# A gated-convolution and differential-attention block: every engine's order from a build-time list scheduler

## The reference

```python
h = rmsnorm(x, g_mix)
bc, cc, vc, q, k, va, gc, ga = split(h @ w_in)     # 512,512,512,512,512,512,1024,1024
y_c = (bc * causal_dwconv3(cc * vc)) @ w_conv_out
q, k = rope(rmsnorm(q)), rope(rmsnorm(k))          # 4 heads, each 2 sub-heads of 64
p0, p1 = softmax(q_n @ k_n.T / 8), masked by chunks of 64 rows
o = (p0 - lam * p1) @ va                           # 4 heads of 128
y_a = (rmsnorm(o) * 0.2) @ w_attn_out
x = x + (sigmoid(gc + b) * y_c + sigmoid(ga + b) * y_a) @ w_o
gt, up = split(rmsnorm(x, g_ffn) @ w_gate_up)      # 2 x 2816
x = x + (silu(gt) * up) @ w_down
```

## Time and profile before

| | us |
|---|---|
| three runs, median | 2865.08 |
| lowest, highest | 2856.92, 2875.99 |
| profiled execution, span of the slowest core | 2843.8 |
| spans of all eight cores | 2839.7 to 2843.8 |

### The profile page before, as it was taken

The page is one execution under the profiler, slowest core; times in us unless marked ns, Lnnn a source line. Parts: engine busy times, 40 slices in busy tenths (PEclk is TensorE's granted clock), DMA queues, the critical chain, the costliest instruction groups (busy, mean ns, idle before and its releaser), DMA issues.

```text
span 2843.8 us, 41548 instructions; the slowest of 8 cores (2839.7 to 2843.8 us)
## 1 busy us (share of the span) xinstructions
PE 2393.0 (84%) x14080; PEld 1110.5 (39%) x14080; DVE 1159.1 (41%) x2138; ACT 1058.7 (37%) x1556; POOL 243.5 (9%) x239
## 2 busy tenths in 40 slices
PE   2566779886997879987899879998799988999989
PEld 1222334333443334433344334443344444444434
DVE  4445544445344443345333453334533333223444
ACT  2134244223323233332443334443355444555310
POOL 1310110003000020001100021000210000000000
PEclk9788799988999889998999999999999999999999
DMA  6336659851335222352234422244122332223333
GB/s 197 106 126 216 222 164 330 297 174 60 113 118 187 97 82 97 121 174 86 82 104 135 156 68 91 99 143 152 60 90 97 118 127 91 82 78 123 134 120 139
DMA packets 107245, 373.61 MB, mean 131 GB/s; under 512 B 10528, under 2 KB 11680, under 8 KB 103072
## 3 DMA queue, kind: packets, MB, share of 16 engines
q1 hardware_dynamic: 106320, 367.81, 38.6%
q10 hardware_dynamic: 720, 3.15, 0.4%
HBM read 320.58 MB, written 50.33 MB: 130 GB/s over the span
## 4 chain that ended last, share of the span: by engine, by line
PE 67%; DVE 13%; issue 8%; ACT 4%; POOL 4%; DMA 3%; DVEq 1%; ACTq 0%; POOLq 0%; SPq 0%
PE psD L817 20%; PE psD L698 12%; PE psO L617 10%; PE psD L844 9%; PE psS L600 6%; PE psD L515 4%; PE psD L764 4%; PE psD L791 3%; DMA kT<-wblk 2%; ACT yq L650 2%; POOL scr L542 2%; DVE scr L645 2%; DVE scr L529 2%; DVE st L532 1%; POOL small L415 1%
## 5 line engine op out<-in xcount | busy, mean ns | idle before, releaser
L606 ACT ACTIVATE Pb<-psS 128x1024 bf16<-128x1024 f32 (+1 forms) x576 | 548.1, 952 | 795.5 <-PE psS L600 774.8
L817 PE MATMUL psD<-hF,wring 128*128 128x512 bf16 x2816 | 666.3, 385 | 10.5 <-DVE hF L426 5.0
L698 PE MATMUL psD<-hT,wring 128*128 128x512 bf16 x1792 | 448.0, 395 | 15.9 <-DVE Pb L609 6.9
L817 PEld LDWEIGHTS psD<-hF,wring 128*128 128x128 bf16 x2816 | 267.0, 99 | 294.0 <-issue 30.1
L617 PE MATMUL psO<-Vs,Pb 128*128 128x129 bf16 x4224 | 351.7, 229 | 3.1 <-DVE Pb L609 3.1
L844 PE MATMUL psD<-wring,big 128*128 128x512 bf16 x1408 | 333.3, 383 | 8.3 <-DVE wring L356 7.7
L515 PE MATMUL psD<-wring,hT 128*128 128x512 bf16 x768 | 245.5, 468 | 76.2 <-DVE scr L538 46.2
L617 PEld LDWEIGHTS psO<-Vs,Pb 128*128 128x128 bf16 x4224 | 256.1, 101 | 123.6 <-issue 114.7
L803 DVE SCALAR_TENSOR_TENSOR xt<-psD,xt 128x512 f32<-128x512 f32 x256 | 176.2, 691 | 272.3 <-PE psD L844 214.7
L825 DVE SCALAR_TENSOR_TENSOR scr<-scr,psD 128x512 f32<-128x512 f32 x176 | 121.1, 688 | 371.9 <-ACT scr L823 345.0
L600 PE MATMUL psS<-qT,kT 64*128 64x512 bf16 (+3 forms) x1152 | 222.1, 382 | 59.0 <-ACT Pb L606 58.9
(11 more groups left out here) (88 smaller groups left out, 1600.3 us busy)
## 6 DMA issues: line engine op xcount, KB each, us to landing
wring<-wsc SPq DMA_DIRECT2D x414, 512.0 KB, 3.3
kT<-wblk SPq DMA_DIRECT2D x32, 1024.0 KB, 10.9
wsc<-wring SPq DMA_DIRECT2D x62, 512.0 KB, 10.9
Vs<-wblk SPq DMA_DIRECT2D x30, 1024.0 KB, 11.0
xt<-x SPq DMA_DIRECT2D x60, 512.0 KB, 8.0
out<-xt SPq DMA_DIRECT2D x32, 512.0 KB, 3.6
wring<-wsc SPq DMA_DIRECT2D x14, 256.0 KB, 2.8
xt<-x ACTq DMA_DIRECT2D x4, 512.0 KB, 13.6
```

The lines of the kernel that those rows point to most:

```text
L606: act(lambda: A.activation(out=Pb[:, pi, :, 0:N], in_=psS[:, :, 0:N], func=AF.Exp, scale=0.125), [("ps", "S")], [("P", pi)])
L698: mm(lambda kc=kc: nc.tensor.matmul(psD[bk][:], lhsT=wv[:, kc, col * 128:(col + 1) * 128], rhs=hT[:, jb, kc, :], start=(kc == 0), stop=(kc ...
L817: mm(lambda kc=kc, gu=gu, bk=bk, wv=wv: nc.tensor.matmul(psD[bk][:], lhsT=wv[:, kc, gu * 128:(gu + 1) * 128], rhs=hF[:, kc, :], start=(kc ...
```

## The change

- **A planner.** `Plan` takes every operation as a task: an engine, a duration from a table (`act_ns`, `dve_ns`, `pool_ns`, `MM = 216.0`), what it reads and writes as values of a class, and a position `pos`. `order()` steps through time as a list scheduler and issues on each free engine the ready task of the lowest position for which the buffers are free; it gives each value its slot (bank, scratch, ring) at that time. PE may not run more than `AHEAD` (14 us of position) in front of the oldest unstarted paced task. The program is then issued in that order; the waits at run time are still semaphores.
- **PSUM.** `psO` keeps 3 banks; the other 5 are one pool `psB`, from which score pairs take 2 adjacent banks and all else takes one.
- **Key tiles in twos.** The scores of two key tiles are asked for together (`hold` on the first keeps other tasks from taking banks), and their PV matmuls (16) form one task one group later.
- **Projections one tile ahead.** The q units of tile j+1 are woven into the first gate stage of tile j, the k units into the second, the v units stand after the output projection; x is loaded and normed one tile ahead. The attention of tile j+1 is spread from the second gate stage of tile j to the end of the first gate stage of tile j+1.
- **Weights.** POOL issues a DMA that reads the float32 block and writes bf16 into the ring (8 slots); no engine casts. In tile 0 all 62 blocks come so, and a third of them is written back; in tile 1 the other 41 are read in float32 again and written back. Tiles 2 to 7 read bf16.
- **Down product.** Four groups of 256 output columns, each over all 22 inner tiles in one bank (352 matmuls of 256 columns), so x is added to 16 times with 256 columns instead of 24 times with 512.
- **Smaller moves.** The rotary tables, the halo copies and the product with B move from DVE to POOL, the first convolution tap from DVE to ACT. The output projection runs by rows first. On DVE, ACT and POOL the last wait rides on the instruction itself.

```diff
 LAM_INIT = 0.8 - 0.6 * math.exp(0.0)
-NSLOT = 6
-NSTG = 4
-
+NBANK, NSLOT, NXT, NXN, NYQ, NP, NSCR, SCW, NSM, NST8 = 5, 8, 4, 4, 6, 4, 7, 514, 12, 4
...
 NHB = 62
-KG = ((0, 8), (8, 16), (16, 22))
+SHORT = tuple(HB_DN + c * 3 + 2 for c in range(4))
+WB_MOD = 3
...
+    DMA_RATE = 290.0
+    DMA_LAT = 1900.0
+    AHEAD = 14000.0
+    SWITCH = 100.0
...
+                for e in ("pe", "act", "dve", "pool", "sp"):
+                    if free_at[e] > now or not ready[e]:
+                        continue
+                    ready[e].sort(key=lambda t: t.pos)
+                    pick = None
...
+                    for t in ready[e]:
+                        if e == "pe" and t.paced and t.pos > limit:
+                            continue
+                        need = []
+                        for v in t.vals:
+                            if v.slot is None:
+                                for w in v.group:
+                                    if w.slot is None and w not in need:
+                                        need.append(w)
+                        if held and any(v.cls == "bank" for v in need):
+                            continue
+                        got = self._free(need)
+                        if got is not None:
+                            pick = t
+                            break
+                        if t.hold and self._free([v for v in need if v.cls != "bank"]) is not None:
+                            held = True
...
+                    if e == "pe":
+                        if (t.kind == "qk") != (last_kind == "qk"):
+                            cost += self.SWITCH
+                        last_kind = t.kind
...
+        psB = es.enter_context(nc.psum_tensor("psB", [128, NBANK, 512], F32))
...
+        def weight(p, b):
+            if (p, b) in wcur:
+                return wcur[(p, b)]
+            v = val("ring")
+            wcur[(p, b)] = v
+            pos = clk["p"] - 40000.0
+            n = 1536 if b in SHORT else 2048
+            early = b % WB_MOD == 0
+            if p == 0 or (p == 1 and not early):
+                dma(lambda: nc.gpsimd.dma_start(out=wring[:, v.slot, 0:n], in_=wblk_d[b][:, 0:n]), [], [(v, 0)], 512 * n,
+                    pos, lambda: ("wc", v.slot), q="pool", strict="w")
+                if (p == 0) == early:
+                    dma(lambda: nc.sync.dma_start(out=wsc_d[b][:, 0:n], in_=wring[:, v.slot, 0:n]), [(v, 0)], [(WSC, b)],
+                        256 * n, pos + 60000.0, lambda: ("cv", v.slot))
+            else:
+                dma(lambda: nc.sync.dma_start(out=wring[:, v.slot, 0:n], in_=wsc_d[b][:, 0:n]), [(WSC, b)], [(v, 0)],
+                    256 * n, pos, lambda: ("wr", v.slot), strict="w")
+            return v
...
+            B = val("bank")
+            B.group = (B,) + also
+            p = 0 if j < 2 else j - 1
+            W = [weight(p, b) for b in hbs]
+            pos = tick(8 * MM)
...
+            pl.add("pe", 8 * MM, subs, pos, soft=soft, kind="proj")
...
+            groups = [(h, g) for h in range(NH) for g in range(nkt // 2)]
...
+            def qk_exp(h, g, at):
+                for kt in (2 * g, 2 * g + 1):
+                    N = n_of(kt)
+                    S1, P = val("bank", n=2), val("P")
+                    S1.group = (S1, P)
+                    PV[(h, kt)] = P
+                    subs = []
+                    for n in range(2):
+                        subs.append((lambda S1=S1, kt=kt, N=N, n=n: PEE.matmul(
+                            bank(S1, n)[:, 0:N], lhsT=kT[n * 64:(n + 1) * 64, h, kt * 128:(kt + 1) * 128],
+                            rhs=qT[n * 64:(n + 1) * 64, QT[j].slot, h, T - N:T], start=True, stop=True),
+                            [(KT, kt)] + [(QT[j], t) for t in range(4 - N // 128, 4)], [(S1, n)]))
+                    pl.add("pe", N / 512.0 * MM, subs, at, hold=(kt % 2 == 0), strict="qk", kind="qk")
+                    act(act_ns(2 * N), lambda S1=S1, P=P, N=N: A.activation(
+                        out=Pb[:, P.slot, :, 0:N], in_=psB[:, S1.slot:S1.slot + 2, 0:N], func=AF.Exp, scale=0.125),
+                        [(S1, 0), (S1, 1)], [(P, 0)], at)
+                    if kt >= 4 * j:
+                        dve(200.0, lambda P=P: V.memset(Pb[64:128, P.slot, :, 0:64], 0.0), [], [(P, 0)], at)
...
+                for kt in (2 * g, 2 * g + 1):
+                    r = max(kt - 4 * j, 0)
+                    P = PV[(h, kt)]
+                    for q in range(r, 4):
+                        for n in range(2):
+                            b, s = o_reg(q, n)
+                            subs.append((lambda kt=kt, P=P, q=q, n=n, b=b, s=s, r=r: PEE.matmul(
+                                psO[:, b, s * VW:(s + 1) * VW], lhsT=Pb[:, P.slot, n, (q - r) * 128:(q - r + 1) * 128],
+                                rhs=Vs[:, kt, h * VW:(h + 1) * VW], start=(kt == 0 and s == 0), stop=(kt == 4 * j + q),
+                                skip_group_check=True), [(VV, kt), (P, 0)], [(O, b)]))
+                pl.add("pe", len(subs) * 56.5, subs, at, kind="pv")
...
+                W = [weight(j, HB_DN + c * 3 + g) for g in range(3)]
+                B = val("bank")
+                ns = NFC * 109.5
+                pos = tick(ns)
+                subs = []
+                for kc in range(NFC):
+                    Wv = W[kc // 8]
+                    subs.append((lambda kc=kc, Wv=Wv: PEE.matmul(
+                        bank(B)[:, 0:256], lhsT=big[:, kc, t * 128:(t + 1) * 128],
+                        rhs=wring[:, Wv.slot, :].rearrange("p (k c) -> p k c", k=8)[:, kc % 8, :],
+                        start=(kc == 0), stop=(kc == NFC - 1)), [(Wv, 0), (act_[kc], 0)], [(B, 0)]))
+                pl.add("pe", ns, subs, pos, kind="down")
...
+        for j in range(NST):
+            nxt = j + 1 < NST
+            if nxt:
+                norm_in(j + 1, clk["p"] + 6000.0, 4000.0)
...
+                q0, k0, v0 = proj_lists(0)
+                q1, k1, v1 = proj_lists(1)
+                weave(v0 + conv + v1, [])
+                for f in q0 + k0:
+                    f()
+                a = clk["p"]
+                for f in q1 + k1:
+                    f()
...
+            weave(gate_list(j, 0, HB_GC, HB_CO, by, mix), q, 3)
...
+            wins.append((att, a, clk["p"] - 8000.0))
+            a = clk["p"]
...
+            weave(gate_list(j, 1, HB_GA, HB_AO, ON[j], mix), k, 1)
+            weave(out_list(j, mix, XR), [])
+            for f in v:
+                f()
+            if nxt:
+                att = attention(j + 1)
+            act_ = {}
+            weave(ffn_list(j, act_), [])
+            weave(down_list(j, act_, XR), [])
...
+            out.append((sem, v))
+        if eng_name in ("dve", "act", "pool") and kind == "c":
+            for sem, v in out[:-1]:
+                eng.wait_ge(sem, v)
+            return out[-1:]
+        for sem, v in out:
             eng.wait_ge(sem, v)
...
-        psS = es.enter_context(nc.psum_tensor("psS", [128, 2, 512], F32))
-        psO = es.enter_context(nc.psum_tensor("psO", [128, 3, 512], F32))
-        NDB = 3
```

More of the change, by code:

```diff
@@ L38, with __init__ @@
 NHB = 62
-KG = ((0, 8), (8, 16), (16, 22))
+SHORT = tuple(HB_DN + c * 3 + 2 for c in range(4))
+WB_MOD = 3
 C_GMIX, C_GFFN, C_BG, C_CW, C_QN, C_KN, C_LAM, C_SN, C_INV, C_END = 0, 8, 16, 32, 44, 108, 172, 428, 429, 461
 CW = 464
+class Val:
+    def __init__(self, cls, slot=None, n=1):
+        self.cls = cls
+        self.slot = slot
+        self.n = n
+        self.touch = 0
+        self.group = (self,)
+        self.turn = None
+class Task:
+    def __init__(self, eng, ns, subs, pos, vals):
+        self.eng = eng
+        self.ns = ns
+        self.subs = subs
+        self.pos = pos
+        self.vals = vals
+        self.succ = []
+        self.ndep = 0
+        self.at = 0.0
+        self.dma = None
+        self.strict = None
+        self.hold = False
+        self.begun = False
+        self.paced = True
@@ new lines, in heap_push, with heap_pop @@
+def heap_push(h, x):
+    h.append(x)
+    i = len(h) - 1
+    while i:
+        p = (i - 1) // 2
+        if h[p] <= h[i]:
+            break
+        h[p], h[i] = h[i], h[p]
+        i = p
+def heap_pop(h):
+    top = h[0]
+    last = h.pop()
+    if h:
+        h[0] = last
+        i = 0
+        while True:
+            c = 2 * i + 1
+            if c >= len(h):
+                break
+            if c + 1 < len(h) and h[c + 1] < h[c]:
+                c += 1
+            if h[i] <= h[c]:
+                break
+            h[i], h[c] = h[c], h[i]
+            i = c
+    return top
@@ L91, in _waits @@
         waits = {}
+        out = []
         for d in deps:
```

1413 lines of the change are left out of this document (735 added, 678 removed).

## The result

The changed kernel takes 2317.7 us (median of five runs, the fastest 2308.3), the kernel before 2865.1; the ratio is 0.808, with a 95% interval of 0.804 to 0.813.

What follows compares the result with a forecast made beforehand. PE, the busiest engine, was taken as the bound, with 749 us lost. Opening 600 plus tiles 2 to 7 at 1754 (1562 work, 5 down product, 50 visits, 137 losses) made span 2354; plus 21.3, 2375 us, range 2290 to 2540.

Steps and rivals of the forecast that it cites:

- Work: PE's matmul work in the whole kernel: 2095 us before, 2101 after, with +6 for the down product in 256 columns.
- Visits: PE's switches to the scores and back: 288 instead of 576, 0.20 us each, 58 us; the second pair costs nothing.
- Opening: Tiles 0 and 1: 600 us instead of 868.6, from PE at 561, DMA at 526 and 39 for mutual waits.
- The rate of the casting DMA: Opening's weight loads: casting taken at the plain rate by bytes read, 313 GB/s, so 164.6 MB take 526 us.
- R1: Opening: casting DMA at half rate or slow POOL issues, from 4.3 us each, keep it near 866; 2641 us, 12%.
- Losses of tiles 2 to 7: PE's lost time there: 137 us instead of 314, from 33 projection, 74 other and 30 for bursts of scores.
- the projection loss: Projection stages in tiles 2 to 7: 33 us lost in each of five, 165 in all, a fifth staying.
- R5: Whole kernel: losses go nearly altogether, opening at 570 and losses 60; 2265 us, 2%.
- The 21.3 us between span and run: Whole kernel: the median run stood 21.3 us above the span before; added to span 2354 to give 2375.
- R3: Scores: the second pair waits for the first's banks, an exp of 1.02 us per burst, +294; 2669 us, 6%.
- R4: Scores: PE waits 2.7 us per burst for both exps and a bank's eviction, 786 us; 3160 us, 3%.
- R2: Tiles 2 to 7: the planned order holds only in part, +50 projection and +50 other losses; 2475 us, 17%.

Runs made afterwards that it cites:

- run 9: Changed kernel with banks held back for both score pairs of a visit instead of the first alone; fastest 2356.6 us, ratio 0.828 to the kernel before.
- run 11: Changed kernel with POOL's third and later weight DMAs waiting until tile 0's fourth x tile has landed; fastest 2318.4 us, ratio 0.814 to before.
- Runs 3 and 10: Changed kernel with float32 stages, ACT and DVE casts, all blocks written back in tile 0: 2366.0 us; changed kernel with only all blocks written back there: 2346.8 us.
- Run 5: Changed kernel with PE allowed only 3 us instead of 14 us ahead of the oldest unit not yet started; fastest 2597.6 us, ratio 0.912.
- single: Changed kernel with one key tile per visit to the scores instead of two; fastest 2341.0 us, ratio 0.822 to the kernel before.
- stage: Changed kernel with q, k and v units as one stage between output projection and FFN, not woven into gate stages; fastest 2344.4 us, ratio 0.823.
- block: A run of a kernel; the text does not say which one carries this name.
- the four layout parts: Planned kernel, 11 us reach, with key tiles in twos, shared score banks, DMA casts and woven projections all undone; fastest 2586.0 us, ratio 0.908.

## Why the prediction was right

**Forecast 2375, measured 2317.7**, inside 2290 to 2540, 57 us (2.4%) high. By its own steps:

- **Work: right.** 2101 us forecast; pace and small steps add up to 2106. The down product in 256 columns cost 4 us of pace, 6 forecast.
- **Visits: the price right, the count wrong.** 58 us for 288 visits; measured 381 visits, of which the account prices 706 of the 762 changes, 69.5 us (at 0.10 each all of them are 76). The price stayed at 0.20 per visit, and the second pair of a visit cost nothing, as taken. But the planner puts other work between the pairs when four banks aren't free; run 9 shows that forcing them together costs more than it saves.
- **Opening: 600 against 605.0, by two errors that cancel.** I kept the opening's work at the 533 us of before. "Projections one tile ahead" takes the projection of one tile out of it: its pace is 507 us, and the missing 24 went into tiles 2 to 7. Against that PE stood 60 us and lost 13 at 1.2 GHz, with 11 ahead of the first matmul, where I had allowed some 57 in all. The start was 27.1 us, not 18. The eight float32 blocks beside the x tiles are not the reason: with six of them held back (run 11) it was 26.0. Why the x tiles land so late stays open. Runs 3 and 10 fit the forecast that DMA and PE tie there: more bytes in tile 0 lengthen it at once, fewer in tile 1 hardly shorten that.
- **The rate of the casting DMA: nearly right.** Taken at the plain rate by bytes read; by the engines' own time it was 308 GB/s against 337, 9% slower, far from the half of R1. On the 105.9 MB that is 30 us of the DMA engines, spread over the opening. The Trainium skill (HBM Reference, Specifications) has 358 GB/s per core; no run here reached it, and with queues full all the time the plain queue's measure gives 337. R1 did not come: an issue holds POOL 0.55 us against the 4.3 at which it would have decided. On the rule of the Trainium skill (SBUF — State Buffer, Who interferes with whom) that VectorE's two-port modes lock GpSimd out: the 103 issues took 554 ns on average and none more than 0.81 us, so a long lock does not show in them.
- **Losses of tiles 2 to 7: the mis-sized term.** 137 us forecast, and 59 measured (1703.9 less 1584.7 of pace and 60.6 of visits), 44 of them standing. It was a guess in fractions: a fifth of the projection loss, half of the rest, 0.1 us for each burst. The projection loss was also counted five times, 165 us, where tiles 2 to 7 of the kernel before hold four such stages (384 of the 768 matmuls of L515 lie behind 868.6 us); with four the same fractions give 147. Four fifths of the 314 us went. Run 5 fits the reading that most of it was of one kind, PE queued behind an unfinished tail: with a short reach such waits come back. This term is 78 us too high; 59 lies below the 80 to 190 of the likeliest case and at the 60 of R5, which had 2%. Pace 18 us and visits 11 us above the forecast make up for a third of it, so part of the closeness of the total is luck.
- **The 21.3 us between span and run: wrong.** They were the spread of the runs, not a fixed addition: the profiled execution of the changed kernel took 2310.5 us with a span of 2308.9, and single, stage and block too are within 2 us of theirs. Against the median, which is 8.8 us above the span, that put 13 us on the forecast.
- **Rivals.** R3 and R4 (bursts waiting for banks) need banks held back; the planner holds them for the first pair alone, and run 9, which holds them for both, loses 48 us, 0.15 us for each of its 311 visits and not 1.0 or 2.7. R2 did not come either: the order held at run time.
- **What the forecast didn't ask: which part makes the gain.** I spread it over parts as if they were independent. With the four layout parts undone the planned kernel is still 264 us faster than before (2586 against 2850 on the same chip), and a short reach alone takes 289 back. In the fixed order the cast brought 27 us and the weave cost some 85. So the list order with its reach carries the largest share that was shown, 289 us, and the parts (33 to 58 us each when undone, the second one on top of the first) are worth more with it. It is not shown that the order makes all of the 264 us: the planned kernel with the four parts undone still has the down product in 256 columns, eight ring slots instead of six, x one tile ahead, the smaller moves and the waits that ride on the instruction, and none of these was undone. How the 115 us of their overlap divides over the four was not taken apart further; some 100 of them lie in tiles 6 and 7, where the longest waits are those of PV for the exp.

## What to carry to other kernels

When PE's lost time is many waits of 2 to 6 us behind tails of its own units, what helped here is an order that knows durations and lets the engine run a dozen us ahead of an unfinished unit (3 us instead of 14 cost 289); moving stages under a fixed order made it worse (+3%). Price a part inside the kernel in which it will live: the cast was worth 27 us in one and 58 in the other, the weave -85 and +36. Two key tiles in one visit save 0.2 us for each visit less, but forcing them together by holding banks back cost more than that (+48 us).

## What the runs showed of the hardware

- A casting DMA (float32 to bf16) from POOL moved 308 GB/s of bytes read per time of all DMA engines, the plain queue 337 (335 in the kernel before); the profile counts its written bytes.
- It held POOL for 554 ns on average per block of 1 MB, 0.81 us at most.
- A change between 64-row score matmuls and 128-row matmuls cost 0.10 us each way; a second score pair straight behind the first started 0.22 us after it, at full pace.
- A matmul of 256 columns kept a pace of 109 ns with a weight load for each.
